# Nine more operand turns by block transposes and DRAM trips, the last down slots by token tile, a 32-column forget gate and later last heads, in a two-block fp32 decoder on one core

## The reference

```python
# block 1
a = rms_norm(x, mix_norm)
h = x + fox_mixer(a)            # 16 heads x 128, a forget gate per head, causal softmax, @ w_out
h = h + conv_ffn(rms_norm(h, ffn_norm))   # @ w_up (2 x 5632), conv of 3 taps, silu(gate) * val, @ w_down
# block 2
h = h + mixer_block(rms_norm(h))  # one w_in of 11264 columns: HGRN2 (8 heads), chunk attention (16 x 64)
                                  # merged = gate_a * (y_a @ w_branch_a) + gate_b * (y_b @ w_branch_b); merged @ w_out
h = h + square(relu(rms_norm(h) @ w_up)) @ w_down   # 8192 wide
return rms_norm(h, norm_final)
```

## Time and profile before

| | us |
|---|---|
| median of 3 runs | 2573.26 (2572.63 to 2573.35) |
| the profiled execution, its own time | 2572.82 |
| its span in the trace | 2570.6 |
| busy: PE, DVE, ACT, POOL | 2545.2 (99%), 1628.3 (63%), 1274.0 (50%), 173.9 (7%) |
| DMA | 530.04 MB, mean 206 GB/s |

### The profile page before, as it was taken

One profiled execution on the slowest core, in us unless ns is written; L12 is line 12 of the kernel. 1 busy time (PEld: TensorE's weight loads), 2 busy tenths in 40 slices (PEclk: granted clock), 3 DMA queues, 4 the chain that ended last, 5 costly groups with the idle time before them and its releaser, 6 DMA issues.

```text
span 2570.6 us, 32628 instructions
## 1 busy us (share of the span) xinstructions
PE 2545.2 (99%) x11604; PEld 2114.7 (82%) x11604; DVE 1628.3 (63%) x1812; ACT 1274.0 (50%) x1609; POOL 173.9 (7%) x289
## 2 busy tenths in 40 slices
PE   8999999999999999999999999999999999999998
PEld 7888888888888888878888888888888888888886
DVE  5666655766666666666677555455565666666665
ACT  5555554655555555554343645454444444444444
POOL 0111100100000000000001000000010000000000
PEclk9999999999999999999999999999999999999999
DMA  7877756877777777755556666665677777777775
GB/s 227 257 204 220 204 170 203 241 225 225 226 223 227 223 223 228 207 170 174 157 151 188 209 194 184 181 191 185 187 238 212 222 211 221 213 219 217 215 219 156
DMA packets 264773, 530.04 MB, mean 206 GB/s; under 512 B 20747, under 2 KB 22131, under 8 KB 264563
## 3 DMA queue, kind: packets, MB, share of 16 engines
q1 hardware_dynamic: 243488, 469.82, 60.7%
q0 software_dynamic: 17152, 54.54, 7.7%
q10 hardware_dynamic: 4051, 4.59, 0.5%
HBM read 501.07 MB, written 27.81 MB: 206 GB/s over the span
## 4 chain that ended last, share of the span: by engine, by line
PE 97%; DVE 1%; DMA 1%; ACT 1%; issue 0%; POOL 0%; ACTq 0%; POOLq 0%; SPq 0%
PE acc L449 31%; PE acc L451 31%; PE acc L450 31%; PE acc L704 1%; PE acc L462 1%; PE acc L557 1%; PE acc L564 0%; DMA scratch<-qk_rows 0%; DVE w_lo L1323 0%; PE acc L579 0%; DVE scratch L1533 0%; DMA raw<-in_w 0%; ACT w_hi L855 0%; PE acc L580 0%; PE acc L741 0%
## 5 line engine op out<-in xcount | busy, mean ns | idle before, releaser
L1323 DVE TENSOR_TENSOR w_lo<-raw,w_hi 128x1024 fp32r<-128x1024 f32 x887 | 1080.4, 1222 | 813.8 <-ACT w_hi L855 811.1
L855 ACT ACTIVATE w_hi<-raw 128x1024 fp32r<-128x1024 f32 x887 | 938.6, 1060 | 1060.3 <-PE acc L451 1001.0
L449 PE MATMUL acc<-w_hi,A_hi 128*128 128x512 f32 x1948 | 769.1, 395 | 0.8 <-issue 0.8
L451 PE MATMUL acc<-w_hi,A_lo 128*128 128x512 f32 x1948 | 758.7, 389 | 0.0
L450 PE MATMUL acc<-w_lo,A_hi 128*128 128x512 f32 x1948 | 758.7, 389 | 0.0
L451 PEld LDWEIGHTS acc<-w_hi,A_lo 128*128 128x128 f32 x1948 | 365.7, 188 | 76.9
L449 PEld LDWEIGHTS acc<-w_hi,A_hi 128*128 128x128 f32 x1948 | 365.9, 188 | 75.8 <-issue 1.4
L450 PEld LDWEIGHTS acc<-w_lo,A_hi 128*128 128x128 f32 x1948 | 365.9, 188 | 73.8
L449 PE MATMUL acc<-w_hi,B_hi 128*128 128x512 f32 x800 | 313.9, 392 | 3.1 <-issue 3.1
L451 PE MATMUL acc<-w_hi,B_lo 128*128 128x512 f32 x800 | 312.1, 390 | 0.0
L450 PE MATMUL acc<-w_lo,B_hi 128*128 128x512 f32 x800 | 311.8, 390 | 0.0
(11 more groups left out here) (184 smaller groups left out, 1240.2 us busy)
## 6 DMA issues: line engine op xcount, KB each, us to landing
raw<-in_up SPq DMA_DIRECT2D x304, 512.0 KB, 4.2
raw<-in_w SPq DMA_DIRECT2D x271, 512.0 KB, 4.1
raw<-in_down SPq DMA_DIRECT2D x216, 512.0 KB, 4.6
raw<-in_wo SPq DMA_DIRECT2D x64, 512.0 KB, 3.9
up_rows<-scratch POOLq DMA_DIRECT2D x21, 512.0 KB, 5.1
scratch<-up_rows POOLq DMA_DIRECT2D x84, 128.0 KB, 5.1
raw<-in_wa SPq DMA_DIRECT2D x16, 512.0 KB, 4.9
raw<-in_wb SPq DMA_DIRECT2D x16, 512.0 KB, 4.7
```

The source lines that it names most:

```text
L449: pe.matmul(o, hi[:, kt, ts], wh, start=first and kk == 0, stop=False)
L451: m = pe.matmul(o, lo[:, kt, ts], wh, start=False, stop=last and kk == SLOT_K - 1)
L855: act.activation(w_hi[:, q % RING, :], raw[:, q % RING, :], ACT.Copy).then_inc(w_hi_ready, 1)
L1323: dve.tensor_tensor(w_lo[:, q % RING, :], raw[:, q % RING, :], f32(w_hi[:, q % RING, :]), ALU.subtract).then_inc(w_lo_ready, 1)
```

## The change

The nine turns become trips. DVE `half_blocks` makes two block transposes (one for each token tile) right after the chunk's end, POOL `half_trip` sends and brings, and each trip's sending waits for the landing of the trip before (`half_back`). Later ACT `operand_back` applies four gains in place (not for the merge) and copies to hi, and DVE `operand_back` subtracts to lo. After fox the blocks are made at slots 14, 16 and 24 and taken up at 20, 23 and 30 (`RES1_AT`); in R5 and R6 at slot 0 and 6 of the next chunk. The forget gate holds hi and lo side by side in 32 columns, so two matmuls for each row tile do. The last group's heads 0 to 3 begin at slots 2, 4, 5, 7 (1, 3, 5, 7 before). The last FFN pass makes its gate steps one or two slots earlier, and its value taps, product and lo part one slot earlier. The final down chunks 2 and 3 are computed tile by tile, and the closing norm follows each token tile, with eight output DMAs of 256 KB. The gain for it is now loaded before R6's trips, and the norm of R6 stands behind them on POOL.

```diff
-        D1_BANKS, D1_TURN, D1_LAST = [BK[2], BK[3], BK[2], BK[3]], [BK[0], BK[3], BK[0], BK[3]], [BK[0], BK[1], BK[0], BK[3]]
+        D1_BANKS, D1_TURN, D1_LAST = [BK[2], BK[3], BK[2], BK[3]], [BK[0], BK[3], BK[0], BK[3]], [BK[1], BK[0], BK[1], BK[3]]
+        RES1_AT = [20, 23, 30]
...
-            at = {"mix": 5, "turn_p": 3, "score": 1, "turn_qk": 0} if last else \
-                 {"mix": 8, "turn_p": 5, "score": 3, "turn_qk": 1}
+            begun = (2, 4, 5, 7) if last else (3, 5, 7, 9)
+            after = {"mix": 4, "turn_p": 2, "score": 0, "turn_qk": -1} if last else \
+                    {"mix": 5, "turn_p": 2, "score": 0, "turn_qk": -2}
...
-                        pe.matmul(o, fw_hi[:, kt, :], A_hi[:, kt, :], start=kt == 0, stop=False)
-                        pe.matmul(o, fw_lo[:, kt, :], A_hi[:, kt, :], start=False, stop=False)
-                        m = pe.matmul(o, fw_hi[:, kt, :], A_lo[:, kt, :], start=False, stop=kt == KT - 1)
+                        pe.matmul(o, fw[:, kt, :], A_hi[:, kt, :], start=kt == 0, stop=False)
+                        m = pe.matmul(o, fw[:, kt, :], A_lo[:, kt, :], start=False, stop=kt == KT - 1)
...
-                for m in range(NCH - 1):
-                    if p == OUT1_END[m] + 2:
-                        pe.wait_ge(res1_out, m + 1)
-                        pe.wait_ge(mixed_lo, FOX_H)
-                        turn(chunk_of_resid(m), TN_RES1 + m)
...
+            def operand_back(n, src, hi, kt, g=None):
+
+                nth = BY_BLOCK.index(n)
+                act.wait_ge(half_back, 64 * (nth + 1))
+                if g is not None:
+                    for j in range(JT):
+                        v = src.rearrange("p (a j e) -> p j a e", a=4, j=JT)[:, j]
+                        m = act.activation(v, v, ACT.Copy, scale=gain[:, g + kt + j:g + kt + j + 1])
+                    chain.link(m)
+                act.activation(in_tokens(hi[:, kt:kt + JT, :]), from_quads(src), ACT.Copy).then_inc(turn_act, 1)
...
+            def half_blocks(n, x, src, ready):
+
+                nth = BY_BLOCK.index(n)
+                dve.wait_ge(*ready)
+                if nth:
+                    dve.wait_ge(half_sent, 16 * nth)
+                for t in range(TT):
+                    m = dve.transpose(block_columns(x, t), src(t).rearrange("p (j b q) -> p j b q", j=JT, b=4))
+                m.then_inc(half_block, 1)
...
+            def half_trip(n, x, dst, free):
+
+                nth = BY_BLOCK.index(n)
+                pool.wait_ge(half_block, nth + 1)
+                if nth:
+                    pool.wait_ge(half_back, 64 * nth)
+                pool.dma_start(turn_rows, x).then_inc(half_sent, 16)
+                pool.wait_ge(half_sent, 16 * (nth + 1))
+                pool.wait_ge(*free)
+                for b in range(4):
+                    pool.dma_start(dst[32 * b:32 * (b + 1), :].rearrange("p (a e) -> p a e", a=4),
+                                   half_by_quad[b]).then_inc(half_back, 16)
```

More of the change, by code:

```diff
@@ L238, in build_program, with on_pe @@
         TN_MERGE, TN_RES2, TN_FFN2 = TN_HG + 6, TN_HG + 10, TN_HG + 14
+        BY_BLOCK = [TN_RES1 + m for m in range(3)] + [TN_MERGE + n for n in range(3)] + [TN_RES2 + n for n in range(3)]
+        def on_pe(n):
+            return n - sum(m < n for m in BY_BLOCK)
         OUT1 = ([(0, k) for k in range(6)] + [(1, k) for k in range(6)] + [(0, 6), (0, 7), (1, 6), (1, 7)]
@@ L841, in _, with last_downs @@
                 pe.wait_ge(down2_out, 4 * i - 1)
-            downs2(R_END - 2, 0, FFN2, (A_hi, A_lo), D2_LAST)
+            def last_downs():
+                H = NCH
+                pe.wait_ge(up2_lo, FFN2)
+                for q in range(H):
+                    gemm(R_END - 2, q, A_hi, A_lo, q % 2, D2_LAST[q // 2], q % 2 == 0, q % 2 == 1)
+                pe.wait_ge(down2_out, 4 * FFN2 - 3)
+                for t in range(TT):
+                    for q in range(H, 2 * NCH):
+                        if t == 0:
+                            pe.wait_ge(w_lo_ready, RING * (R_END - 2) + q + 1)
+                        o, ts = acc[:, D2_LAST[q // 2][t], :], slice(t * P, (t + 1) * P)
+                        for kk in range(SLOT_K):
+                            wh, wl = (w[:, q % RING, kk * CW:(kk + 1) * CW] for w in (w_hi, w_lo))
+                            kt, last = q % 2 * SLOT_K + kk, q % 2 == 1 and kk == SLOT_K - 1
+                            pe.matmul(o, A_hi[:, kt, ts], wh, start=q % 2 == 0 and kk == 0, stop=False)
+                            pe.matmul(o, A_hi[:, kt, ts], wl, start=False, stop=False)
+                            m = pe.matmul(o, A_lo[:, kt, ts], wh, start=False, stop=last)
+                        if q % 2 == 1:
+                            m.then_inc(tile_done, 1)
+            last_downs()
         @block.scalar
@@ L1300, in _, with square_tile, square_both @@
                     up2_operand(FFN2 - 1, A_hi)
[L1301 to L1311 removed]
+            def square_tile(t, c):
+                act.wait_ge(last_added, 2 * t + c - 1)
+                m = act.activation(junk[:, :], resid[:, t, c * CW:(c + 1) * CW], ACT.Square, scale=D ** -0.5,
+                                   accum_out=final_ssq[:, t, c:c + 1])
+                m.then_inc(last_squared, 1)
+                act.wait_ge(last_squared, 2 * t + c - 1)
+            def square_both(c):
+                act.wait_ge(down2_out, 4 * (FFN2 - 1) + c + 1)
+                for t in range(TT):
+                    m = act.activation(junk[:, :], resid[:, t, c * CW:(c + 1) * CW], ACT.Square, scale=D ** -0.5,
+                                       accum_out=final_ssq[:, t, c:c + 1])
+                    if t < TT - 1:
+                        chain.link(m)
+                m.then_inc(squares, 1)
+                act.wait_ge(squares, 4 * NCH + c + 1)
+            for q in range(NCH + 1):
+                split(R_END - 2, q)
+                if q in (1, 4):
+                    square_both(q // 4)
+            for t in range(TT):
+                square_tile(t, 2)
+                square_tile(t, 3)
+                act.wait_ge(last_rstd, t + 1)
+                act.wait_ge(gained, 2)
+                for c in range(2):
+                    v = resid[:, t, c * CW:(c + 1) * CW]
+                    act.activation(v, v, ACT.Copy, scale=rstd[:, t:t + 1]).then_inc(scaled_act, 1)
         @block.vector
@@ L1425, in first_steps @@
                     dve.wait_ge(rstd_ready, 1)
-                    for t in range(TT):
-                        v = slice(t * FOX_H, (t + 1) * FOX_H)
-                        m = dve.scalar_tensor_tensor(out=f_logit[:, v], in0=acc[:, 6, T:T + TT * FOX_H][:, v],
-                                                     scalar=rstd[:, t:t + 1], in1=f_bias, op0=ALU.mult, op1=ALU.add)
+                    for half in range(2):
+                        for t in range(TT):
+                            v = f_logit[:, t * FOX_H:(t + 1) * FOX_H]
+                            col = T + (2 * t + half) * FOX_H
+                            m = dve.scalar_tensor_tensor(out=v, in0=acc[:, 6, col:col + FOX_H], scalar=rstd[:, t:t + 1],
+                                                         in1=v if half else f_bias, op0=ALU.mult, op1=ALU.add)
+                        if half == 0:
+                            chain.link(m)
                     m.then_inc(f_z, 1)
@@ L1663, in _ @@
                     dve.wait_ge(levels_made, 1)
[L1664 removed]
+                    dve.wait_ge(filled, 5)
                 step = hg_step(p)
```

207 lines of the change are left out of this document (126 added, 81 removed).

## The result

| | before | after |
|---|---|---|
| median of 8 runs, us | 2573.31 (2571.75 to 2577.43) | 2580.1 (2575.39 to 2584.61) |
| span of the profiled execution | 2570.6 | 2578.5 |
| its own time | 2572.82 | 2580.31 |
| PE busy | 2545.2 | 2539.3 |

What follows compares the result with a forecast made beforehand. PE's program plus its waits was taken to bound the kernel. Gains of 18.7 us less 7.8 for the trips gave -10.9, so 2572.8 became 2561.9, with a median of 2562.4 us; range 2553.5 to 2568.

Steps and rivals of the forecast that it cites:

- the forget gate: Forget gate on PE: 16 fewer matmuls at 0.117 us each, a gain of 1.9 us.
- the end of R3 with the clock and the start of R4: PE's waits there shrink: 2.8 us at R3's end, 1.5 for the clock, 0.8 before R4's first matmul.
- a turn: PE's transposes of a chunk: each turn costs 0.89 us, so removing nine gains 8.0 us.
- The queue after fox: Three chained residual trips after fox make PE wait 3T - 33.6, here 6.3 us; with the clock 7.8.
- T: Length of one trip, taken as 13.3 us for all nine; forecast allowed 11.8 to 14.6.
- The clock: Lower granted clock on PE behind the wait after fox, at the start of R3: a cost of 1.5 us.
- The merge has one more 1.2 us operation before and no gains: S + 20.6, 1.2 of room. These six trips cost nothing: Trips in R5 and R6: hidden behind eight PE slots at T = 13.3, cost 0; S is the next chunk's start.
- After R6 the same step: Residual trips after the merge: blocks end 3.75 us into the next chunk, 0.7 us of room, no wait.
- the tail: Behind the last matmul: half-size chain and small output DMAs end the kernel 3.3 us sooner (2.3 to 4).
- the heads: Last heads: head 0's 1.68 us wait goes, a new 1.3 us wait comes before head 2; net gain 0.4.
- (D): Rival, slower: T of 16.6 us or more at all three stages costs over 5.1 us; chance 0.03.
- (E): Rival: heads, R3's end and the clock there give nothing, 5.5 us less gain, time 2567.9; chance 0.05.

Runs made afterwards that it cites:

- experiment 7: Changed kernel with every landed chunk taken up later, last heads at the old places, last root by exp and logarithm on ACT: 2560.53 us, ratio 0.9944.
- experiment 8: Kernel before, with its last scale factors made by a reciprocal on DVE instead of two operations on POOL: 2572.15 us, ratio 0.9994.
- experiment 1: Changed kernel with the three residual chunks after fox turned on PE again: 2570.34 us, ratio 0.9992.
- experiment 4: Changed kernel with the last two scale factors made by a reciprocal on DVE instead of a power on POOL: 2572.31 us, ratio 0.9987.
- experiment 10: Experiment 9 with one more POOL instruction at the end, a write of a small tile nobody reads: 2553.44 us, 2.7 us more than experiment 9.
- Experiment 6: Changed kernel with last heads begun at slots 2, 4, 6, 8 and mixes needed only by the slots that read them: 2572.09 us, ratio 0.9998.
- experiment 9: Experiment 7 with last heads at slots 2, 4, 6, 8 and last root as square root on ACT plus reciprocal on DVE: 2550.73 us, ratio 0.9917.
- experiment 2: Changed kernel with a second DRAM tensor and landing semaphore for the second trip after fox: 2574.64 us, ratio 1.0005.
- experiment 5: Changed kernel with the last group's heads begun at slots 1, 3, 5, 7 again: 2576.08 us, ratio 1.0014.

## Why the prediction was wrong

**Right in kind and size:** the forget gate (1.9, measured 2.0), the end of R3 with the clock and the start of R4 (5.1, measured 4.9). The lo part was no longer the last to come there; PE now waited 0.8 for the chunk sum on DVE, which the text had taken off its path (of the experiments with the changed R3, only experiment 7's trace has such a wait over 0.4). The share of the clock in the 4.9 was in part luck: in experiment 8, the kernel before with the same wait of 3.1 us, the clock stayed at full behind it, and the step there was 1.6 us less than in the earlier trace rows's trace.

**Right in kind, mis-sized:** a turn costs PE 0.80 and not 0.89 (7.2, not 8.0). The queue after fox: 3T - 33.6 with T = 13.3 gave 6.3, measured 8.3. The three trips took 13.4, 14.0 from its sending, and 14.1, 13.8 on average, and with that the formula gives 7.9. The other 0.4 is nearly the 0.55 between the first landing and the second sending (368.61 to 369.16), which the text had at nothing. So the form was right, and T = 13.3 was 0.5 short, which counts three times, as the text said. The clock cost 1.8, not 1.5.

**Wrong, the step "The merge has one more 1.2 us operation before and no gains: S + 20.6, 1.2 of room. These six trips cost nothing".** I followed one chunk's trip by itself. I had written the rule down for the stage after fox, that what stands behind a waiting take-up on DVE is late, and didn't apply it in R5: there the sums that start the next trip stand behind the take-up of the last. With T above 13.8 the delays of three trips add up. Measured: a wait of 5.7, and 8.4 with the clock behind it. The size has two causes. By the text's own formula, one trip by itself with 1.2 of room at T = 13.3, the last trip's 16.0 would have cost 1.5; the loop made it 5.7. And with T = 13.3 the loop gives 39.9 - 41.5, so no wait either: had the trips been as short as I took them, the missing loop would not have shown. Between experiment 1 and the changed kernel the mean T grew by 1.8 us, and the cost, with the clock, from 0.8 to 8.4.

**After R6 the same step, in small.** The trips took 13.9 to 14.0, for which the text priced nothing. But the third chunk's sum stands behind the second's take-up there too. DVE, timeline, in the changed kernel:

```profile
1844.57 1.22 DVE L1407 TENSOR_TENSOR B_lo<-scratch,B_hi 128x1024 fp32r<-128x1024 f32 x1 [2.48 <-ACT B_hi L932]
...
1846.85 1.22 DVE L1435 TENSOR_TENSOR resid<-resid,acc 128x1024 f32<-128x1024 f32 x1
...
1849.12 1.30 DVE L1417 STREAM_TRANSPOSE scratch<-resid 128x512 f32<-128x512 f32 x2
```

PE had finished that chunk at about 1844.95, so the blocks end 5.5 us behind it and not 3.75, and the 0.7 of room became 1.9 late.

**Wrong, T itself in R5.** My three rows of T gave 10.7, 13.3 and 15.9, and I took the middle one for all nine. The trips in R5 took 15.2 to 16.2 in the changed kernel's trace, 13.7 to 16.2 in the experiments'. The middle of three rows is no bound for nine trips, and where a loop stands behind it, its spread sets the cost.

**Wrong, the tail.** The chain to the last landing was right (12.3 to 8.5, 3.8 us), but the end of the program is not the last landing. The step "the last landing comes about 3.3 us sooner" took the span's end for that. Experiments 4 and 10 show that POOL's drain holds it.

**Wrong, the heads.** I had put the new wait at 1.3 and it was 1.1, and head 0 kept 0.5 of its own. I had missed the wait of 1.3 at a mix: head 2's mix needs head 1's lo part from DVE, and that waits for ACT, which takes another head's exp and a split first. Experiment 6 gives what the later start is worth with even spacing.

Of the rivals, (D) came nearest in outcome, slower, but not by its mechanism: it asked for T of 16.6 everywhere. (E) named the heads. The loop in R5 and the drain were in no rival.

Open stays why trips in R5 are mostly longer than those after R6; the bytes of the weight stream are the same for both. That a sending close behind other brings lands later (8.0 against 3.8 us) was seen in one place.

## What to carry to other kernels

When work is taken off the bounding engine and sent on a trip with a length that varies, look on every engine at what stands behind the instruction that waits for it, above all whether the start of the next trip stands there. Take a landing up at the last place that its reader allows, behind the work that others wait for, and let the reader wait for each piece alone. That, with the heads and the tail mended too, turned a loss of 0.3% into a gain of 0.8%: of the 29 us between the changed kernel and experiment 9, about 8 are the heads and the tail. Look at the very last rows of a trace, at which queue the others wait for, before pricing an edit of the tail.

## What the runs showed of the hardware

POOL's drain at the end of a program took 8.4, 9.7 and 9.3 us from the start of its last instruction on (kernel before, after, experiment 10), whatever that instruction was, a write of a small tile too; with DMA sendings last it took 12.2 to 13.3 us (experiments 4, 7, 8 and 9). SP's took 0.007 us. The drain set the end where POOL's last instruction started 6.1 and 5.9 us before the last landing (changed kernel, experiment 10); in the kernel before it was 8.2.

The clock stood at its lower level (granted 0.50, 1.2 GHz instead of 2.4) behind waits of 5.5 and 5.7 us in the changed kernel, and at the higher one behind those of 0.8, 1.8 and 2.6. The length of the wait alone does not decide it: it was 0.50 or 0.51 behind waits of 1.8 (experiment 2, before the MLP), 2.0 (experiment 4), 2.5 (experiments 5 and 7) and 3.1 us, and 1.00 behind those of 2.8 (experiments 2 and 6) and 3.1 us (experiment 8). So a price for the clock that is put on a wait of 2 to 3 us can come or not.
